# Sample attention of a hybrid decoder layer: scores and page sums spread over four column groups of TensorE, and a scan cut in four

## The reference, cut to what matters

```python
def attend_sample(q, k_new, v_new, lam, k_past, v_past):      # 8 samples, PAST = 256 = 2 pages of 128
    s_past = einsum('bqhmd,bkhmd->bhmqk', q, k_past) * scale  # two 64-wide maps m of each head
    s_new = einsum('bqhmd,bkhmd->bhmqk', q, k_new) * scale
    p = softmax(concatenate([s_past, s_new], axis=-1))        # 257 columns
    w = p[:, :, 0] - lam * p[:, :, 1]
    return einsum('bhqk,bkhd->bqhd', w[..., :P], v_past) + einsum('bhqk,bkhd->bqhd', w[..., P:], v_new)

def hgrn2_recurrence(q, k, v, log_f, s0):                     # per chunk of tokens
    b = cumsum(log_f)                                         # restarts at every chunk
    q_dec = q * exp(b); a = tril(q_dec @ (k * exp(-b)).T)
    o = a @ v + q_dec @ S
    S = exp(b_last) * S + (k * exp(b_last - b)).T @ v
```

## Time and profile before

| | us |
|---|---|
| median of 3 runs | 2974.2 (2973.12 to 2978.13) |
| the profiled execution, its own time | 2973.09 |
| its span, first to last instruction | 2971.3 |
| PE busy in the span | 2909.2 (98%) |
| PEld busy | 2670.5 (90%) |
| DVE busy | 1499.3 (50%) |
| ACT busy | 1068.2 (36%) |
| POOL busy | 96.4 (3%) |
| the stage over the heads | about 70 to 1065 |

### The profile page before, as it was taken

The page is one execution under the profiler, slowest core; times in us unless marked ns, Lnnn a source line. Parts: engine busy times, 40 slices in busy tenths (PEclk is TensorE's granted clock), DMA queues, the critical chain, the costliest instruction groups (busy, mean ns, idle before and its releaser), DMA issues.

```text
span 2971.3 us, 53260 instructions
## 1 busy us (share of the span) xinstructions
PE 2909.2 (98%) x19995; PEld 2670.5 (90%) x19995; DVE 1499.3 (50%) x2411; ACT 1068.2 (36%) x1481; POOL 96.4 (3%) x75
## 2 busy tenths in 40 slices
PE   6999999999999999999999999999999999999998
PEld 6888888888888899899999999999999999998998
DVE  5455453554444645544554444544445545455544
ACT  4355454454543523422233222332223322234332
POOL 2011010110100100000000000000000000000000
PEclk9999999999999999999999999999999999999999
DMA  5333333333333533233233332333322323323332
GB/s 196 93 105 98 96 96 97 106 99 88 94 103 101 172 113 86 80 92 92 85 92 94 92 92 84 93 96 90 92 87 88 102 85 92 92 84 93 99 106 85
DMA packets 546618, 291.78 MB, mean 98 GB/s; under 512 B 15208, under 2 KB 537570, under 8 KB 546378
## 3 DMA queue, kind: packets, MB, share of 16 engines
q1 hardware_dynamic: 515482, 268.88, 31.0%
q10 hardware_dynamic: 31040, 21.46, 2.3%
HBM read 268.83 MB, written 21.63 MB: 98 GB/s over the span
## 4 chain that ended last, share of the span: by engine, by line
PE 92%; DVE 4%; ACT 2%; issue 2%; SPq 0%; DMA 0%; DVEq 0%; ACTq 0%
PE product L883 26%; PE product L887 14%; PE product L885 14%; PE product L884 14%; PE product L886 13%; PE scratch L698 2%; PE scratch L706 2%; PE scratch L747 1%; DVE w_lo L1429 1%; PE scratch L792 1%; PE scratch L769 1%; PE scratch L752 1%; ACT L1057 1%; PE scratch L697 1%; DVE r_km L1632 1%
## 5 line engine op out<-in xcount | busy, mean ns | idle before, releaser
L883 PE MATMUL product<-act,w_hi 128*128 128x512 f32 x2816 | 1151.6, 409 | 37.1 <-DVE act L1656 15.0
L1429 DVE TENSOR_TENSOR w_lo<-w_raw,w_hi 128x1024 fp32r<-128x1024 f32 (+1 forms) x496 | 607.5, 1226 | 580.2 <-ACT w_hi L1046 580.1
L1046 ACT ACTIVATE w_hi<-w_raw 128x1024 fp32r<-128x1024 f32 (+1 forms) x496 | 514.2, 1037 | 978.7 <-PE product L887 957.0
L887 PE MATMUL product<-act,w_lo 128*128 128x264 f32 x2816 | 808.0, 287 | 0.0
L885 PE MATMUL product<-act,w_hi 128*128 128x264 f32 x2816 | 803.3, 285 | 0.0
L884 PE MATMUL product<-act,w_hi 128*128 128x264 f32 x2816 | 802.2, 285 | 0.0
L886 PE MATMUL product<-act,w_lo 128*128 128x256 f32 x2816 | 794.6, 282 | 0.0
L885 PEld LDWEIGHTS product<-act,w_hi 128*128 128x128 f32 x2816 | 533.1, 189 | 128.7
L883 PEld LDWEIGHTS product<-act,w_hi 128*128 128x128 f32 x2816 | 535.8, 190 | 55.3 <-issue 22.2
L884 PEld LDWEIGHTS product<-act,w_hi 128*128 128x128 f32 x2816 | 535.6, 190 | 3.4 <-issue 1.9
L887 PEld LDWEIGHTS product<-act,w_lo 128*128 128x128 f32 x2816 | 534.6, 190 | 0.0
(11 more groups left out here) (249 smaller groups left out, 2526.6 us busy)
## 6 DMA issues: line engine op xcount, KB each, us to landing
w_raw<-in_w_in SPq DMA_DIRECT2D x112, 512.0 KB, 3.8
w_raw<-in_w_gate SPq DMA_DIRECT2D x88, 512.0 KB, 3.8
w_raw<-in_w_up SPq DMA_DIRECT2D x88, 512.0 KB, 3.8
w_raw<-in_w_down SPq DMA_DIRECT2D x64, 384.0 KB, 3.4
w_raw<-in_w_down SPq DMA_DIRECT2D x64, 320.0 KB, 3.2
w_raw<-in_w_out SPq DMA_DIRECT2D x32, 512.0 KB, 3.9
w_raw<-in_w_ple_gate SPq DMA_DIRECT2D x32, 384.0 KB, 3.4
k_pages<-in_cache_k SPq DMA_DIRECT2D x128, 64.0 KB, 2.8
```

What stands on the lines that cost most here:

```text
L883: pe.matmul(both, hi, x[:, k, :, 0:TA], start=begin, stop=False)
L887: mm = pe.matmul(far, lo, x[:, k, 1, TA:T], start=False, stop=end)
L1046: act.activation(w_hi[:, slot, 0:n, :], w_raw[:, slot, 0:n, :], ACT.Copy).then_inc(w_hi_ready, 1)
L1429: dve.tensor_tensor(flat(w_lo[:, slot, 0:n, :]), flat(w_raw[:, slot, 0:n, :]), flat(w_hi[:, slot, 0:n, :]).bitcast(F32), ALU.subtract).the ...
```

## The change: what it does

- Output rows of the samples' tasks are spread over the four groups of 32 columns of the PE array (which are the four groups of 32 partitions of PSUM). Sample y adds into rows 32j to 32j+31 with j = y mod 4; `q_pad` gets blocks of 32 columns, cut from a row of cells 34 apart that GpSimd zeroes once, and DVE writes only the 16 cells that are not zero, in two copies in place of one product.
- The softmax then runs over 128 rows, most of them of no meaning, in place of 16.
- `s_prob` turns pieces of 128 x 128 by the transpose; DVE picks the pairs of columns out with one reduction for each page of the two.
- `s_out` sends page y to group y mod 4. The first four matmuls take 32 columns of `w_pad`, so that all 32 rows of the group are written; the others take 8.
- `s_turn` becomes a matmul of `s_o` (128 x 128) with a table `sum_groups` (128 x 8) that adds the four groups while it turns.
- The scan runs as four scans of 128 elements; the table `restart` is dropped, and so is `pad_q`. The load of the tables goes from 2660 to 2028 columns.

```diff
             elif name == "s_score":
                 for y in range(NS):
-                    mm = pe.matmul(M[b][0:16, 0, 0:PAST + 1], q_pad[:, y, :], kT[:, y, :], start=y == 0, stop=y == NS - 1)
+                    j = y % COL_GROUPS
+                    mm = pe.matmul(M[b][j * GROUP_ROWS:(j + 1) * GROUP_ROWS, 0, 0:PAST + 1], q_pad[:, y, :], kT[:, y, :],
+                                   start=y < COL_GROUPS, stop=y >= NS - COL_GROUPS)
...
             elif name == "s_prob":
                 for y in range(2):
-                    turn(M[b][:, 0, y * 16:(y + 1) * 16], s_p[:, y * P:(y + 1) * P], 16)
-                turn(M[b][0:16, 1, 0:P], v_two[:, :], P).then_inc(full[b], 1)
+                    turn(M[b][:, 0, y * SPREAD:y * SPREAD + P], s_p[:, y * P:(y + 1) * P], P)
+                turn(M[b][:, 1, 0:P], v_two[:, 0:P], P).then_inc(full[b], 1)
             elif name == "s_out":
-                out = M[b][0:NS, 0, 0:P]
                 for y in range(NPG):
-                    pe.matmul(out, w_pad[:, y, :], v_pages[:, y, :], start=y == 0, stop=False)
-                pe.matmul(out, new_w[:, :], new_v[:, :], start=False, stop=True).then_inc(full[b], 1)
+                    j = y % COL_GROUPS
+                    if y < COL_GROUPS:
+                        w, rows = flat(w_pad[:, y:y + GROUP_ROWS // NS, :]), GROUP_ROWS
+                    else:
+                        w, rows = w_pad[:, y, :], NS
+                    pe.matmul(M[b][j * GROUP_ROWS:j * GROUP_ROWS + rows, 0, 0:P], w, v_pages[:, y, :],
+                              start=y < COL_GROUPS, stop=y >= NPG - COL_GROUPS + 1)
+                pe.matmul(M[b][0:NS, 0, 0:P], new_w[:, :], new_v[:, :], start=False, stop=True).then_inc(full[b], 1)
             elif name == "s_turn":
-                turn(M[b][:, 0, 0:NS], s_o[:, :], NS).then_inc(full[b], 1)
+                pe.matmul(M[b][:, 0, 0:NS], s_o[:, :], K("sum_groups"), start=True, stop=True).then_inc(full[b], 1)
...
-                    dve.tensor_tensor(q_pad[:, :, :], q_rot[:, SEQ:T].unsqueeze(2).broadcast_to([P, NS, 16]),
-                                      K("pad_q").rearrange("p (b c) -> p b c", b=NS), ALU.mult).then_inc(flag("q_pad_done"), 1)
+                    for m_ in range(2):
+                        half = slice(m_ * DK, (m_ + 1) * DK)
+                        t = dve.tensor_copy(q_cells[half, :, m_:m_ + 1].rearrange("p b o -> p (b o)"), q_rot[half, SEQ:T])
+                    t.then_inc(flag("q_pad_done"), 1)
...
-                dve.tensor_copy(v_two[:, :].rearrange("p (b w) -> p b w", w=2),
-                                z_v[:, SEQ:T].unsqueeze(2).broadcast_to([P, NS, 2])).then_inc(flag("v_two_done"), 1)
+                for m_ in range(2):
+                    t = dve.tensor_copy(pair_columns(v_two[:, :])[:, :, :, m_:m_ + 1].rearrange("p a j o -> p a (j o)"),
+                                        z_v[:, SEQ:T].rearrange("p (a j) -> p a j", j=COL_GROUPS))
+                t.then_inc(flag("v_two_done"), 1)
...
-                dve.tensor_reduce(w_sum[:, :], M[b][:, 0, 0:32].rearrange("p (x w) -> p x w", w=2), AX.X, ALU.add).then_inc(flag("w_sum_done"), 1)
-                dve.tensor_copy(new_v[0:16, :], M[b][0:16, 1, 0:P]).then_inc(free[b], 1)
+                for g in range(PAGES):
+                    t = dve.tensor_reduce(w_sum[:, g * NS:(g + 1) * NS].rearrange("p (a j) -> p a j", j=COL_GROUPS),
+                                          pair_columns(M[b][:, 0, g * SPREAD:(g + 1) * SPREAD]), AX.X, ALU.add)
+                t.then_inc(flag("w_sum_done"), 1)
+                dve.tensor_copy(new_v[:, :], M[b][:, 1, 0:P]).then_inc(free[b], 1)
...
-                    dve.tensor_tensor_scan(r_b[:, :], K("restart"), r_kh[:, :], 0.0, ALU.mult, ALU.add).then_inc(flag("scan_done"), 1)
+                    for j in range(BLOCKS_T):
+                        t = slice(j * P, (j + 1) * P)
+                        scan = dve.tensor_tensor_scan(r_b[:, t], K("ones"), r_kh[:, t], 0.0, ALU.mult, ALU.add)
+                    scan.then_inc(flag("scan_done"), 1)
...
-                nc.gpsimd.memset(new_w[:, :], 0.0).then_inc(flag("zeros_set"), 1)
-                nc.gpsimd.memset(new_v[:, :], 0.0).then_inc(flag("zeros_set"), 1)
+                nc.gpsimd.memset(q_padded[:, :], 0.0).then_inc(flag("zeros_set"), 1)
+                nc.gpsimd.memset(v_two[:, :], 0.0).then_inc(flag("zeros_set"), 1)
```

More of the change, by code:

```diff
@@ L65 @@
 KC = 8
+COL_GROUPS = 4
+GROUP_ROWS = P // COL_GROUPS
+GROUP_STEP = GROUP_ROWS + 2
+SPREAD = COL_GROUPS * GROUP_STEP
 DOWN_TILES = (6, 5)
@@ L176 @@
                   ("swap", P), ("ones64", P), ("cos", T), ("sin", T),
-                  ("causal", SEQ), ("restart", SEQ), ("pairs_in", P),
-                  ("pad_q", NS * 16), ("delta8", NS * NS), ("delta_p", NS), ("pairs", NS),
+                  ("causal", SEQ), ("pairs_in", P),
+                  ("sum_groups", NS), ("delta8", NS * NS), ("delta_p", NS), ("pairs", NS),
                   ("coef", 2), ("maps", 2)):
@@ L215, in constants @@
     put("causal", causal)
-    put("restart", np.tile((np.arange(SEQ) % P != 0).astype(np.float32), (P, 1)))
     put("pairs_in", (p[:, None] <= p[None, :]).astype(np.float32))
[L218 to L222, removed]
+    put("sum_groups", (p[:, None] % GROUP_ROWS == np.arange(NS)[None, :]).astype(np.float32))
     put("delta8", np.tile(np.eye(NS, dtype=np.float32).reshape(1, -1), (P, 1)))
     put("delta_p", np.eye(NS, dtype=np.float32))
-    put("pairs", (np.arange(16)[:, None] // 2 == np.arange(NS)[None, :]).astype(np.float32))
-    put("coef", np.stack([np.arange(16) % 2 == 0, -(np.arange(16) % 2.0)], 1).astype(np.float32))
+    group, row = p // GROUP_ROWS, p % GROUP_ROWS
+    put("pairs", ((row[:, None] // 2 == np.arange(NS)[None, :]) & (group[:, None] == np.arange(NS)[None, :] % COL_GROUPS)).astype(np.float32))
+    put("coef", np.stack([p % 2 == 0, -(p % 2.0)], 1).astype(np.float32))
     put("eps", np.full((P, 1), EPS, np.float32))
@@ L290, in program @@
     v_nat = hb("v_nat", [P, 5, P])
-    coef = hb("coef", [16, 1])
+    coef = hb("coef", [P, 1])
     lb = hb("lb", [P, HEADS])
@@ L308, in program @@
     v_pages = k_pages
-    q_pad = hb("q_pad", [P, NS, 16])
-    s_p = hb("s_p", [16, PAST + 1])
-    s_stat = hb("s_stat", [16, 5])
+    q_padded = hb("q_pad", [P, NS * GROUP_STEP])
+    q_pad = q_padded[:, 0:NS * GROUP_ROWS].rearrange("p (b c) -> p b c", b=NS)
+    q_cells = q_padded[:, :].rearrange("p (b c) -> p b c", b=NS)
+    s_p = hb("s_p", [P, PAST + 1])
+    s_stat = hb("s_stat", [P, 5])
     w_sum = hb("w_sum", [P, NPG])
     w_pad = hb("w_pad", [P, NPG, NS])
-    s_o = hb("s_o", [NS, P])
-    v_two = hb("v_two", [P, 16])
+    s_o = hb("s_o", [P, P])
+    v_two = hb("v_two", [P, SPREAD])
     new_w = hb("new_w", [P, NS])
@@ L1117, in small @@
                 b = take(name, it, [("s_max_done", n)])
-                func(s_p[:, :], M[b][0:16, 0, 0:CP], ACT.Exp, scale=SCALE, bias=s_stat[:, 1:2],
+                func(s_p[:, :], M[b][:, 0, 0:CP], ACT.Exp, scale=SCALE, bias=s_stat[:, 1:2],
                      accum_out=s_stat[:, 2:3]).then_inc(free[b], 1)
@@ L1125, in small @@
                 b = take(name, it)
-                func(s_o[:, :], M[b][0:NS, 0, 0:P], ACT.Copy).then_inc(free[b], 1)
+                func(s_o[:, :], M[b][:, 0, 0:P], ACT.Copy).then_inc(free[b], 1)
             elif name == "s_turn":
@@ L1715, in visit @@
                 dve.wait_ge(flag("setup_d"), 2)
-                dve.scalar_tensor_tensor(coef[:, :], K("coef")[0:16, 1:2], lam[0:16, 0:1], K("coef")[0:16, 0:1], ALU.mult, ALU.add).then_inc(flag("setup_d"), 1)
+                dve.scalar_tensor_tensor(coef[:, :], K("coef")[:, 1:2], lam[:, 0:1], K("coef")[:, 0:1], ALU.mult, ALU.add).then_inc(flag("setup_d"), 1)
                 dve.tensor_tensor(lbt[:, 2, :], lbt[:, 0, :], lbt[:, 1, :], ALU.add).then_inc(flag("setup_d"), 1)
```

4 lines of the change are left out of this document (2 added, 2 removed).

## The result

The changed kernel takes 2927.7 us in the median (2924.4 to 2930.5) and the kernel before 2973.75: ratio 0.984, 95% interval 0.9825 to 0.9859, so 46 us or 1.6% less. The forecast was 2946.6 with a range of 2937 to 2973.

What follows compares the result with a forecast made beforehand. PE was taken to bound the kernel; 8 x (1.43 + 1.65 + 0.42 + 0.18) = 29.4 us saved, less 1.8 for the scan, gave 27.6 us and a median of 2946.6, range 2937 to 2973.

Steps and rivals of the forecast that it cites:

- What bounds the kernel: PE, busy 98% of the span: a nanosecond less PE work saves a nanosecond, unless PE then waits.
- `s_score` and `s_out`: Passes overlap in pairs across groups, 9 turns for 16 and 18 for 34; saves 1.43 and 1.65 us a head.
- the loads ahead: Weight loads before first passes at `s_score` and `s_out`, charged 0.2 us at the most and 0.1 us.
- more than two at once: Rival: passes needn't wait for the one before in the program; `s_score` and `s_out` shrink, 2928 us; 10%.
- its 9 turns at `s_out`: Under the rival with more than two at once, `s_out` takes 9 turns, saving 25 x 0.109 us.
- `s_prob`: Three full-width transposes take 0.45 us in place of 0.87, saving 0.42 us a head without group overlap.
- `s_turn`: Two full-width passes replace the turn, 0.34 us for 0.53; saves 0.10 to 0.29 us a head, 0.18 taken.
- No pause at a change of group: At `s_score` and `s_out`, changing column group doesn't empty the array; the rival that it does: 2993 us, 7%.
- The scan: Four scans on DVE's path cost 0.22 us more a head, 1.8 us in all.
- No new wait: Shorter `s_score` and `s_out` make no split late; the tightest, chunk 12, has 0.61 us of slack.
- stretches at the low clock: Rival: `s_score` or `s_out` brings a half-clock stretch of some 3.4 us in each head, 2974 us; 3%.
- its upper saving: Best case of the prediction's own range: no loads in the way and a free scan, 31.5 us less, 2943.

Runs made afterwards that it cites:

- the order 0, 4, 1, 5: Changed kernel with both passes' samples reordered: two matmuls of a group in a row in `s_score`, four in `s_out`; 2943.5 us, ratio to before 0.988.
- `s_out` alone: Kernel before with only the changed `s_out` and `s_turn`, scores left in one group; 2948.5 us, ratio 0.9906.
- `intra` shortened: Changed kernel with `intra` cut into pieces of 32 stationary columns, each in its rows' group; 2904.7 us, also 2904.7 in a second kernel with two scans.
- three in a row: Changed kernel with `s_out` in group order 0,0,0,1,1,1,2,2,2,3,3,3,0,1,2,3; a single run took 2932.7 us.
- two by two: Changed kernel with groups 0 and 1 in turn, then 2 and 3, in `s_score` and `s_out`; 2929.4 us, ratio to before 0.985.
- the scan alone: Kernel before with only the scan cut in four; 2972.9 us against 2974.6, ratio 0.999.

## Why the prediction was wrong, point by point

- **What bounds the kernel: right.** PE's saved work came out as saved time: 5.73 us in the length of a head for 5.73 from the tasks and the scan.
- **`s_score` and `s_out`: the wrong step.** The prediction had "The second pass of a sample must wait until its first has streamed", which holds; and from PE starting matmuls "in the order of the program" it took that this pass holds up the samples behind it. In the trace of before all neighbours share a group, so their order there says nothing about neighbours in different groups. The runs show in its place that all four groups run at once: a pass waits for the one before it in its own group only, and a matmul behind it in the program goes ahead as long as each group has no more than one waiting. By that count `s_score` has 4 pass times, 4 x 0.218 + 0.13 = 1.00, and `s_out` 10, since group 0 has four pages and `new_w`, two passes each: 10 x 0.109 + 0.12 = 1.21. These are 1.15 and 0.95 us a head less than forecast, 8 x 2.1 = 17 of the 19 us by which the median was missed. The price of the loads ahead (0.2 and 0.1 us) was too high as well: four groups start 0.007 us apart, and beyond the pause of 0.09 only 0.03 or 0.04 us are left for the first loads.
- **The rival "more than two at once"** had the right time, 2928, with a chance of 10%. It was put low for a reason that the trace couldn't bear, and the range was cut so that it fell outside. Its mechanism was right; that it came within 1 us is partly luck. It has 5.34 us a head for the two tasks (5.18 measured; its 9 turns at `s_out` should be 10), and 0.09 too little for `s_turn` and 0.07 too much for the scan make up for it. The Trainium skill ("TensorE: Matmul & The Clock Gate", Part 3) gives 2.38 for three tiles, which spoke for that side (the page doesn't say whether its matmuls were in two passes, as the prediction has it that they were not); here 16 passes went from 3.49 us to 0.91, 3.8 for four groups. Its sentence that matmuls start in strict order, on which the count leaned, is not what the run with the order 0, 4, 1, 5 shows: there four passes start within 0.05 us, so sample 1 begins before sample 4, which stands ahead of it.
- **`s_prob`: right** (0.43 against 0.42). **`s_turn`**: 0.27 against 0.18. Its two passes took 938.15 - 938.01 = 0.14 us, not the 0.22 taken from `s_rnn`. The load of `att_out` stayed exposed: by counting in windows its second pass starts 0.19 us after its first (0.22 before), the next ones 0.11 apart.
- **No pause at a change of group: right.** The pauses of 0.09 us are still at both ends of `s_out` and none is inside. The rule of the Trainium skill that was cited for it ("TensorEngine Tiling (Array Packing)", Key Properties) holds in these runs.
- **The scan**: on the path, as forecast; 0.15 us more, not 0.22.
- **No new wait: right**, also with `s_out` alone and with `intra` shortened. No more stretches at the low clock came either, four in the stage over the heads before and three after.
- **The prediction's own range**: its upper saving, 31.5 us, doesn't come out of its terms, which give 31.0 with 0.18 for `s_turn` and 31.9 with 0.29. Nothing hangs on it.

## What to carry to other kernels

Matmuls of up to 32 stationary columns that follow one another are worth dealing out to the four column groups in turn, fp32 ones too: 16 passes took a quarter of the time here. The order need not be strict, but no group's third matmul should stand ahead of another group's first. Two of a group in a row cost 0.02 us; the order 0, 1, 0, 1 up to the fourth page of each, before 2 and 3, cost 0.27, though no two of a group are neighbours. Give each group the same number, too: the one extra matmul of group 0 is 0.22 us of the 1.21 of `s_out`. For an effect of tenths of a microsecond, measure one round of the loop at full clock, not the whole time. Where a bound rests on an order seen in a trace, ask first whether the trace had a case in which the order could have been another; if not, both ends belong in the range.

## What was not expected of the hardware

Between executions the granted clock moves the time by as much as some parts of the change. It falls to half (0.50, the lower of the two levels, 1.2 GHz) for stretches of 3.4 or 6.8 us, often in or right behind `intra`. In the kernel with four of a group in a row such a stretch stood there in nearly every head. Windows, with the columns of the earlier trace rows:

```profile
892.70:896.10 3.40, 3.40 (x16) 3.20 (x15) 2.32 (x4) 0.00 (x0) 0.00 (x0) 0.50 0.00 0
```

`intra` began there at 889.54. A stretch of 3.4 us costs 1.5 us and one of 6.8 us 3.0 by the length of a head: 120.69 and 122.16 us in the kernel before (from the scans at 644.17 and 522.01) in place of 119.15. The prediction had 3.4 for the long one.

Between 200 and 930 us the profiles have three such stretches before, two after, six with four in a row, four with three in a row, three with two by two, one with `s_out` alone, none with the scan alone and none in the two kernels with the short `intra`. That does not show that a short `intra` avoids them. The kernel with the scan alone has the long `intra` and none either, and the two with the short one have a stretch each at 171 and at 935 us, within 1.5 us behind a wait of PE of 2.1 and 3.2 us; the changed kernel has such a one at 399, behind a wait of 1.8. What decides it from one execution to the next stays open. The twelve times of the kernel with the scan alone spread over 6 us, which is why its 1.2 us can't be seen in them.
